# Transformer block on one core: each stage's first chunk multiplied with the high parts first, fewer idle matmuls, context's parts a chunk later

## The reference, cut to what matters

```python
u = modulate(rms_norm(h), shift, scale)          # before every stage
y = differential_attention(u_lat, u_ctx)         # layer 0, context tokens as keys and values too
h = h + gate * rms_norm(y)
h = h + gate * rms_norm(square(relu(u @ w_in)) @ w_out)     # MLP, 1024 -> 4096 -> 1024
# layer 1: the same around a Hyena mixer: projections, short convolution,
#          long two-sided convolution by Fourier products, then (v * x0) @ w_out
# block 2: rms_norm, one wide projection into four branches (gated MLP, linear recurrence,
#          sparse attention, pooling), gates, w_out; rms_norm, router, 16 experts; rms_norm
```

## Time and profile before

| | us |
|---|---|
| median of 3 runs | 1739.28 |
| lowest, highest run | 1736.54, 1741.97 |
| profiled execution, its time | 1741.85 |
| profiled execution, its span | 1740.1 |
| TensorE, VectorE, ScalarE busy in the span | 1642.2, 1137.5, 763.0 |
| mean granted TensorE clock, share of full | 0.971 |

### The profile page before, as it was taken

One profiled execution on the slowest core, in us unless ns is written; L12 is line 12 of the kernel. 1 busy time (PEld: TensorE's weight loads), 2 busy tenths in 40 slices (PEclk: granted clock), 3 DMA queues, 4 the chain that ended last, 5 costly groups with the idle time before them and its releaser, 6 DMA issues.

```text
span 1740.1 us, 29309 instructions
## 1 busy us (share of the span) xinstructions
PE 1642.2 (94%) x12199; PEld 1516.4 (87%) x12199; DVE 1137.5 (65%) x1558; ACT 763.0 (44%) x888; POOL 11.5 (1%) x25
## 2 busy tenths in 40 slices
PE   6999789999999889999999999999989999999997
PEld 3899667899998776899998999988989999999996
DVE  6966773577678657555557346666555665878786
ACT  2422253355333332456433235544433333767664
POOL 0000000000000000000001000000000000000000
PEclk9899799999999999999999899999998999999999
DMA  8444430266686422234567244422332444778783
GB/s 332 173 170 153 161 121 25 97 225 241 240 306 216 162 97 73 76 133 178 194 224 253 107 161 170 146 95 100 146 127 97 176 166 183 281 299 308 298 307 115
DMA packets 43512, 310.23 MB, mean 178 GB/s; under 512 B 5239, under 2 KB 5624, under 8 KB 6984
## 3 DMA queue, kind: packets, MB, share of 16 engines
q1 hardware_dynamic: 41760, 301.75, 47.3%
q0 software_dynamic: 1248, 5.72, 1.0%
q10 hardware_dynamic: 392, 1.12, 0.2%
HBM read 307.53 MB, written 1.05 MB: 177 GB/s over the span
## 4 chain that ended last, share of the span: by engine, by line
PE 78%; DVE 14%; ACT 4%; issue 2%; DMA 1%; ACTq 0%; SPq 0%; DVEq 0%
PE ps L632 16%; PE ps L634 15%; PE ps L633 15%; PE ps L638 4%; PE ps L640 4%; PE ps L639 4%; DVE macc L1921 3%; DVE wlo L1909 3%; ACT whi L1424 2%; PE ps L689 1%; PE ps L690 1%; PE ps L691 1%; PE ps L1289 1%; PE ps L1363 1%; PE ps L849 1%
## 5 line engine op out<-in xcount | busy, mean ns | idle before, releaser
L1909 DVE TENSOR_TENSOR wlo<-raw,whi 128x2048 fp32r<-128x2048 f32 x218 | 497.8, 2288 | 291.0 <-ACT whi L1424 290.6
L632 PE MATMUL ps<-uhi,whi 128*128 128x256 f32 x1728 | 502.1, 291 | 13.5 <-DVE ulo L1951 4.2
L1424 ACT ACTIVATE whi<-raw 128x2048 fp32r<-128x2048 f32 x218 | 415.9, 1910 | 200.0 <-PE ps L634 143.1
L634 PE MATMUL ps<-ulo,whi 128*128 128x256 f32 x1728 | 494.3, 286 | 0.0
L633 PE MATMUL ps<-uhi,wlo 128*128 128x256 f32 x1728 | 494.3, 286 | 0.0
L632 PEld LDWEIGHTS ps<-uhi,whi 128*128 128x128 f32 x1728 | 337.3, 195 | 23.0 <-issue 16.6
L633 PEld LDWEIGHTS ps<-uhi,wlo 128*128 128x128 f32 x1728 | 337.3, 195 | 1.1 <-issue 1.0
L634 PEld LDWEIGHTS ps<-ulo,whi 128*128 128x128 f32 x1728 | 336.8, 195 | 0.0
L632 PE MATMUL ps<-hid_hi,whi 128*128 128x256 f32 x512 | 145.2, 284 | 1.6 <-ACTq L1608 1.6
L634 PE MATMUL ps<-hid_lo,whi 128*128 128x256 f32 x512 | 144.0, 281 | 0.0
L633 PE MATMUL ps<-hid_hi,wlo 128*128 128x256 f32 x512 | 143.9, 281 | 0.0
(11 more groups left out here) (466 smaller groups left out, 2810.0 us busy)
## 6 DMA issues: line engine op xcount, KB each, us to landing
raw<-weights_in SPq DMA_DIRECT2D x258, 1024.0 KB, 4.8
y<-weights_in SPq DMA_DIRECT2D x18, 1024.0 KB, 5.3
mstart<-mod_start_in SPq DMA_DIRECT2D x4, 2048.0 KB, 19.7
w1c<-cmp_w_in POOLq DMA_DIRECT2D x1, 2048.0 KB, 13.0
h<-x_in SPq DMA_DIRECT2D x1, 1024.0 KB, 7.8
ctx<-ctx_in SPq DMA_DIRECT2D x1, 1024.0 KB, 18.6
y<-decay_in ACTq DMA_DIRECT2D x1, 1024.0 KB, 4.8
out<-y SPq DMA_DIRECT2D x4, 256.0 KB, 2.2
```

Of the source, the lines that this page charges most:

```text
L632: mm(o, w0, x0, start=first, stop=False, **kw)
L634: return mm(o, w0, x1, start=False, stop=last, **kw)
L1424: fn(whi[:, sl, :], raw_at(i) if n is None else raw[:, sl, :], ACT.Copy).then_inc(s("hi_ready"), 1)
L1909: tt(wlo[:, sl, :], raw_at(i) if n is None else raw[:, sl, :], f32(whi[:, sl, :]), ALU.subtract).then_inc(s("lo_ready"), 1)
```

## The change

1. A new helper, `tiles_hi_first`, serves the first chunk of each stage. One matmul with a column of zeros, broadcast over the bank's 512 columns, opens the bank for both tiles; then the 32 products with high parts come, k-tile by k-tile and both tiles in each, waiting for the high parts by quarters; then the 16 with low parts, waiting for the low ones.
2. It is used for the first queries, attention's output rows, both MLPs (there for slot 0 in every turn of the loop), the Hyena input and output rows, the mixer input, the merged branches. The router's products are ordered alike, with an opening of their own.
3. Idle matmuls: 6 to 4, 13 to 9 (three times), 12 to 9, 14 to 11. Those before the queries, the merged branches and between stages stay.
4. ScalarE marks the MLP's free banks ahead of the high parts. VectorE's weighing of the modulation chunk that fell between attention's output rows and the first MLP's norm moves behind the low parts (`late`).
5. Context's high and low parts are made after the first chunk's drain and after the next split, not ahead of them.
6. The convolution's banks are swapped, so that the output rows' first bank is free early; TensorE waits for `conv_taken` before them, and for the last Hyena drain only before bank 0.
7. The router's weights are split into parts ahead of the root and the norm. `zero` is allocated for the whole kernel.

```diff
+            def by_parts(step, tag, k):
+                for c, part in cuts(tag, step):
+                    if part.start == k:
+                        pe.wait_ge(*nth(tag, step, c + 1))
+
+            def open_bank(o, w):
+                mm(o, w, zero[:].to_broadcast([P, o.shape[1]]), start=True, stop=False)
+
+            def tiles_hi_first(i, bank, x0, x1, hi_part, lo_part):
+                sl = i % RING
+                o = [ps[:, bank, m * T:(m + 1) * T] for m in range(2)]
+                wk = lambda w, k, m: w[:, sl, k * 256 + m * P:k * 256 + (m + 1) * P]
+                open_bank(ps[:, bank, :], wk(whi, 0, 0))
+                for k in range(KT):
+                    hi_part(k)
+                    for m in range(2):
+                        mm(o[m], wk(whi, k, m), x0[:, k, :], start=False, stop=False)
+                        mm(o[m], wk(wlo, k, m), x0[:, k, :], start=False, stop=False)
+                for k in range(KT):
+                    lo_part(k)
+                    for m in range(2):
+                        ins = mm(o[m], wk(whi, k, m), x1[:, k, :], start=False, stop=k == KT - 1 and m == 1)
+                return ins
...
-            idle_work(3, 6)
-            out_rows("post0", I_AO, x_wait=head_parts)
+            idle_work(3, 4)
+            out_rows("post0", I_AO, lambda i: tiles_hi_first(i, 0, uhi, ulo, head_parts("o_hi"), head_parts("o_lo")))
...
-                idle_work(6, 13)
+                idle_work(6, 9)
...
-                        used(tiles(i, lambda m, _: ps[:, g, m * T:(m + 1) * T], [(uhi, ulo)], x_wait=tag + "_in" if g == 0 else None))
+                        used(tiles(i, lambda m, _: ps[:, g, m * T:(m + 1) * T], [(uhi, ulo)]) if g else stage_first(i, g, tag + "_in"))
...
-        CONV_BANKS = ((2, 3, 4, 5), (6, 7, 0, 1))
+        CONV_BANKS = ((4, 5, 0, 1), (6, 7, 2, 3))
...
-                if half:
-                    pe.wait_ge(s("hy_drained"), 12)
                 for k in range(4):
+                    if CONV_BANKS[half][k] == 0:
+                        pe.wait_ge(s("hy_drained"), 12)
...
-            out_rows("post1", I_HO, x_wait="hy")
+            pe.wait_ge(s("conv_taken"), 4)
+            out_rows("post1", I_HO, lambda i: stage_first(i, 0, "hy"))
...
-            idle_work(6, 14)
-            pe.wait_ge(*nth("moe_in", "lo", 4))
+            idle_work(6, 11)
             pe.wait_ge(s("router_lo"), 1)
-            for t0 in range(TT):
+            open_bank(ps[:, 4, 0:64], whi[:, I_MOE % RING, 0:P])
+            for part in ("hi", "lo"):
                 for k in range(KT):
...
-            high("ctx", ctx, ctx_hi, mod_scale(0, 0, 1))
...
                 split(i + RING)
+                if g == 0:
+                    high("ctx", ctx, ctx_hi, mod_scale(0, 0, 1))
...
-                high(tag + "_in", y, uhi, mod_scale(layer, 3, 0))
                 slots, turns, rest, body = mlp_plan(layer)
                 act.drain().then_inc(s("mlp_free"), slots)
+                high(tag + "_in", y, uhi, mod_scale(layer, 3, 0))
...
-            low("ctx", ctx, ctx_hi, ctx_lo, mod_scale(0, 0, 1))
...
+                if g == 0:
+                    low("ctx", ctx, ctx_hi, ctx_lo, mod_scale(0, 0, 1))
...
             postnorm("post0", 2)
-            split(I_AO + 3 + RING)
...
-            late = []
+            late = [I_AO + 3]
...
                 dve.drain().then_inc(s("mlp_hidden"), slots)
+                for i in late:
+                    split(i + RING)
+                late.clear()
```

More of the change, by code:

```diff
@@ L676, in tiles, with stage_first @@
                 return ins
+            def by_parts(step, tag, k):
[19 more added lines that the diff above has]
+                return ins
+            def stage_first(i, bank, tag):
+                return tiles_hi_first(i, bank, uhi, ulo, lambda k: by_parts("hi", tag, k), lambda k: by_parts("lo", tag, k))
             def by_token(i, out_of, xs, ncols=256):
@@ L896, in _, with head_parts, wait, out_rows @@
             spread_head_roots()
-            def head_parts(k):
-                if k % 2 == 0:
-                    pe.wait_ge(s("o_lo"), k // 2 + 1)
-            def out_rows(tag, i0, xs=(uhi, ulo), x_wait=None):
+            def head_parts(step):
+                def wait(k):
+                    if k % 2 == 0:
+                        pe.wait_ge(s(step), k // 2 + 1)
+                return wait
+            def out_rows(tag, i0, first):
                 for g in range(4):
                     weights_ready(i0 + g)
-                    used(tiles(i0 + g, lambda m, _: ps[:, g, m * T:(m + 1) * T], [xs], x_wait=x_wait if g == 0 else None))
+                    used(tiles(i0 + g, lambda m, _: ps[:, g, m * T:(m + 1) * T], [(uhi, ulo)]) if g else first(i0))
                 sum_quarters(tag, 4)
-            idle_work(3, 6)
-            out_rows("post0", I_AO, x_wait=head_parts)
+            idle_work(3, 4)
+            out_rows("post0", I_AO, lambda i: tiles_hi_first(i, 0, uhi, ulo, head_parts("o_hi"), head_parts("o_lo")))
             idle_work(6, 10)
@@ L969, in _ @@
                 weights_ready(I_HY + g)
[L970 removed]
+                used(tiles(I_HY + g, lambda m, _: ps[:, g % 2, m * T:(m + 1) * T], [(uhi, ulo)]) if g else stage_first(I_HY, 0, "hy_in"))
                 if g == 0:
@@ L1177, in _ @@
                 weights_ready(I_WO + g)
-                used(tiles(I_WO + g, lambda m, _: ps[:, g, m * T:(m + 1) * T], [u_parts], x_wait="merged" if g == 0 else None))
+                used(tiles(I_WO + g, lambda m, _: ps[:, g, m * T:(m + 1) * T], [u_parts]) if g else stage_first(I_WO, 0, "merged"))
             idle_work(6, 3)
             sum_quarters("moe_in", 5)
-            idle_work(6, 14)
-            pe.wait_ge(*nth("moe_in", "lo", 4))
+            idle_work(6, 11)
             pe.wait_ge(s("router_lo"), 1)
-            for t0 in range(TT):
+            open_bank(ps[:, 4, 0:64], whi[:, I_MOE % RING, 0:P])
+            for part in ("hi", "lo"):
                 for k in range(KT):
-                    a0, a1 = (x[:, k, t0 * P:(t0 + 1) * P] for x in u_parts)
-                    ins = three_rows(mm, ps[:, 4, t0 * 32:t0 * 32 + 20], a0, a1, wrhi[:, k, :], wrlo[:, k, :], k == 0, k == KT - 1)
+                    by_parts(part, "moe_in", k)
+                    for t0 in range(TT):
+                        o, a = ps[:, 4, t0 * 32:t0 * 32 + 20], slice(t0 * P, (t0 + 1) * P)
+                        if part == "hi":
+                            mm(o, uhi[:, k, a], wrhi[:, k, :], start=False, stop=False)
+                            mm(o, uhi[:, k, a], wrlo[:, k, :], start=False, stop=False)
+                        else:
+                            ins = mm(o, ulo[:, k, a], wrhi[:, k, :], start=False, stop=k == KT - 1 and t0 == 1)
             ins.then_inc(s("router"), 1)
@@ L1811, in _ @@
                 fn(sq[:, part, :], h[:, part, :], ACT.Square).then_inc(s("squares"), 1)
-            root("moe_in", 5)
             act.wait_ge(s("router_loaded"), 64)
             fn(wrhi[:], wr[:], ACT.Copy).then_inc(s("router_hi"), 1)
+            root("moe_in", 5)
             high("moe_in", y, uhi)
```

15 lines of the change are left out of this document (7 added, 8 removed).

## The result

The changed kernel takes **1728.28 us** (median of 4 runs, 1727.45 to 1728.45) beside 1737.97 of the kernel before on the same chip: a ratio of 0.9924, 95% interval 0.9907 to 0.9941, or 13.2 us of 1737.97 (10.3 to 16.2). The prediction said 15.9 us and, against the median it was given, 1723.4; the range 1714 to 1733 holds the result. The profiled execution took 1728.45 us with a span of 1726.7, for 1741.85 and 1740.1.

What follows compares the result with a forecast made beforehand. TensorE, busy 94% of the span, bounds the kernel, so only its useless stretches could give time back. Gains at stage starts and router, less openings, summed to 15.9 us: 1723.4 against the median 1739.28, range 1714 to 1733.

Steps and rivals of the forecast that it cites:

- The starts: Gains (us): Hyena input 2.3, second MLP 2.6, mixer input 2.3, first MLP 5.1, convolution's output 2.0, attention's output 0.6.
- TensorE's old start, less the end of the first high quarter, less 0.12: Formula for a stage start's gain; 0.12 us is the hand-over to TensorE after ScalarE's first quarter of high parts.
- rival 1: VectorE or ScalarE can't deliver third and fourth chunks sooner, so leads are given back: 7 us, 1730; chance 0.13.
- the first queries: At the queries' start: a TensorE wait goes, but VectorE does the same work and is late next; gain 0.
- The convolution: Convolution's output rows: opening, 16 products, wait, 16 more, then 16 low ones; 2.0 us gained.
- The openings: Bank openings in 7 later turns of the MLP loops, 0.24 us each: -1.7 us (bounds -0.8 and -6.1).
- it stands after the wait for weights that ends a turn and is therefore not hidden: MLP loops: the reason each turn's opening was charged its full 0.24 us.
- The router: Router: shorter idle work lets the narrow products begin 2.9 us sooner; gain 2.9 us.
- I let that stretch move with them: Router: the half-clock stretch of 4.13 + 6.11 us was assumed to move with the narrow products; gain 2.9 us.
- rival 4: Router's narrow products end before the clock falls, or shared phases turn out well: 4.6 us and more, 1716; chance 0.08.
- Rival 2: Pauses or short idle work make the clock fall at six other starts: 8 us lost, 1731; chance 0.07.
- 2 to 3 us each way: Allowance for clock phases in the forecast's own spread of 1718 to 1729.

## Why the prediction was right, and where not

**The starts.** The steps that carry the forecast are all there: 2.44, 2.58, 2.37, 5.25, 2.03 and 0.67 us for 2.3, 2.6, 2.3, 5.1, 2.0 and 0.6. "TensorE's old start, less the end of the first high quarter, less 0.12" was good to 0.15 us each time. Making the high products wait for low parts removed the gain at four of them and 2.2 us of the first MLP's; putting the weighing back took 1.16 of that one. Nothing of the leads went back to the ring (rival 1), except where the prediction said so, in the first queries.

**The convolution.** The two halves of the high parts show as predicted: 16 products, a pause, 16 more; the pause is 0.80 us. Timeline of after, for the earlier trace rows:

```profile
694.11 0.57 PE L686 MATMUL ps<-zero,whi 128*128 128x512 f32 x1
696.27 1.06 ACT L1705 ACTIVATE uhi<-hv 128x1024 fp32r<-128x1024 f32 x1 [4.94 <-DVE hv L2292]
697.38 0.38 PE L697 MATMUL ps<-uhi,whi 128*128 128x256 f32 x1 [0.80 <-ACT uhi L1705]
```

**The openings** were mis-sized: -1.7 us in the sum, -0.87 in the second MLP and about -0.1 in the first by the run without them. The single cost (0.22 for 0.24) was right; "it stands after the wait for weights that ends a turn and is therefore not hidden" was not, for the first MLP. The row it leaned on the earlier trace rows is a wait in the middle of a turn, behind the opening, and that wait is what hides it.

**The router** was mis-sized the other way: 6.94 for 2.9. Timeline of after (TensorE), for the earlier trace rows, and the half clock that is left:

```profile
1287.35 5.08 PE L645 MATMUL ps<-con 128*128 128x256 f32 x22
1292.30 0.26 PE L1225 MATMUL ps<-wrhi,uhi 128*128 128x20 f32 x1
1295.87 1.93 PE L1228 MATMUL ps<-wrhi,ulo 128*128 128x20 f32 x16
1297.66 0.36 PE L632 MATMUL ps<-uhi,whi 128*128 128x256 f32 x1
```
```profile
1297.90:1301.30 3.40, 3.40 (x18) 3.40 (x18) 2.85 (x19) 0.21 (x1) 0.00 (x0) 0.50 0.58 224
```

The start is 3.8 us earlier (1304.59 less 1292.30, less the lead of 8.5 that was there), the narrow products take 5.4 us instead of 7.35 because they all run at full clock, and the chunk behind them has 3.4 us at half clock instead of 6.1. "I let that stretch move with them" was the step that failed: rival 4 happened here. The start itself is 0.9 us better than forecast, which goes with the clock too: the first 1.4 us of before's idle work ran at half clock (a stretch of 6.8 us from 1290.7), of after's only 0.3 (3.4 us from 1284.3). The surplus is there in both profiled executions of this kernel but not robust: in the variants that leave the router alone the same step is 2.7 to 4.0, except in two, where it is 6.9 again.

**What the sum left out** took the surplus away. Half-clock stretches appeared in the attention (-2.7) and in the experts' stage (-1.6), where the change edits nothing; the latter for one:

```profile
1448.10:1451.50 3.40, 3.40 (x19) 3.40 (x18) 2.23 (x3) 1.02 (x2) 0.00 (x0) 0.50 0.27 65
```

The variants with their own timing have such steps elsewhere or not at all: in the attention -2.71 with the changed kernel, -0.01 with `zero` in 64 bytes, -0.01 with the weighing put back. Rival 2 looked for the clock at the starts, where it did no harm; it struck in stages without an edit. The prediction counted "2 to 3 us each way" for it; here it took 4.3. And the address of `zero`, which item 7 of the change names only as an allocation for the whole kernel, cost 2.5 to 3 us in the dense stages: 1.05 in the queries' chunks, 1.27 in the second MLP's output rows, the rest in the first's. For the queries' chunks that is in part argued, since 64 bytes took back only some 0.7 of it. The prediction costed the move of an allocation at nothing without naming it.

So the total, 13.2 us for 15.9, rests on starts that were right, and in part on luck: errors that the sum did not foresee cancelled, the router's surplus (+4.0) and the openings' (+0.7) against the clock (-4.3, and the start's -0.7) and the addresses (-3).

## What to carry to other kernels

Where a product is split into high and low parts that come from two engines, order the first chunk by when the parts come; the gain of a start could be read here from one row of each engine to 0.15 us. Idle work that keeps the clock up should end just ahead of the new start: four matmuls more cost 1.3 to 1.4 us each time, none at all brought half clock behind the start. Whoever adds a tile, however small, moves the others: keep the addresses in the comparison, and try a padding of 32 bytes ahead of the moving operands, since here it was worth as much as the whole rearrangement.

## What the runs showed of the hardware that I had not expected

- The distance of fp32r products (128x128 weights, 256 columns) changes with the start address of the moving operand, the weights being at 0 modulo 128 bytes: 120.0 ns at 0 and 118.3 at 96 (5.760 and 5.680 us for 48), mostly 116.7 at 32 and 117.8 at 64 (5.600 and 5.653 us). The last two are not fixed by the address: at 32 there are chunks, and in one kernel nearly a whole stage, at 117.8, and at 64 a few chunks at 113.3. The Trainium skill ("SBUF — State Buffer", section "Operand start alignment") asks for a multiple of the element size and calls this a matter of legality, not speed; its runs timed nothing. All addresses here keep that rule, and the speeds differ. What in the chip makes the difference, and whether 128 is the true period, stays open.
- An opening matmul of 512 columns, one column of zeros broadcast, pushes the next product by 0.22 us among dense ones.
- Stretches at half clock lay at the same places in two profiled executions of the changed kernel (within 0.1 us once their different start is taken off, the stretch at the very end apart). Yet kernels that differ by an edit of 1 to 3 us have stretches of 3.4 or 6.8 us moved, added or removed, some of them hundreds of us from the edit. Whether the shift of the work does this or the execution isn't separated, since each variant has one profile and runs of one kernel differ in their granted clock (0.970 to 0.976). A single edit of under 3 us can't be judged by the total here, only by the chunk ends.
